# Three attentions by pairs of heads: V as the stationary operand in two column halves of TensorE, and probabilities divided before they are turned

## The reference, cut to what matters

```
scores = einsum("bqhd,bkhd->bhqk", q_blk, k) * scale      # 8 heads, 96 wide, 512 keys
scores = where(k_idx <= q_idx, scores, -inf)
probs  = softmax(scores, axis=-1)
out    = einsum("bhqk,bkhd->bqhd", probs, v)              # 64 wide
```

## Time and profile before

| what | us |
|---|---|
| median of three runs | 3442.46 (3441.18 to 3444.32) |
| profiled execution, in all | 3443.18 |
| its span, first to last instruction | 3441.5 |
| PE busy | 3358.2 (98%) |
| DVE, ACT, POOL busy | 1790.0, 1471.7, 1433.9 |
| mean granted TensorE clock | 0.997 of full speed |

### The profile page before, as it was taken

One profiled execution on the slowest core, in us unless ns is written; L12 is line 12 of the kernel. 1 busy time (PEld: TensorE's weight loads), 2 busy tenths in 40 slices (PEclk: granted clock), 3 DMA queues, 4 the chain that ended last, 5 costly groups with the idle time before them and its releaser, 6 DMA issues. The chain is left out here.

```text
span 3441.5 us, 49476 instructions
## 1 busy us (share of the span) xinstructions
PE 3358.2 (98%) x19319; PEld 2796.6 (81%) x19319; DVE 1790.0 (52%) x3313; ACT 1471.7 (43%) x2970; POOL 1433.9 (42%) x1268
## 2 busy tenths in 40 slices
PE   8999999999999899999999999999999999999999
PEld 7778778888877687888888878888888878888887
DVE  4655574636456674565463286455153186445243
ACT  4672354323344554532333347344343246544343
POOL 3320154454443545444544431345554432345543
PEclk9999999999999999999999999999999999999999
DMA  4210024545321122344443220222323220123321
GB/s 117 78 44 15 27 86 135 196 147 170 99 89 50 36 88 88 111 149 168 159 147 111 84 74 14 74 86 92 104 83 101 91 79 26 50 86 98 98 92 56
DMA packets 232836, 317.89 MB, mean 92 GB/s; under 512 B 9909, under 2 KB 149148, under 8 KB 232604
## 3 DMA queue, kind: packets, MB, share of 16 engines
q1 hardware_dynamic: 203206, 261.55, 23.6%
q10 hardware_dynamic: 29398, 53.17, 4.6%
HBM read 312.59 MB, written 2.10 MB: 91 GB/s over the span
## 5 line engine op out<-in xcount | busy, mean ns | idle before, releaser
L364 PE MATMUL banks<-split,split 128*128 128x512 f32 (+2 forms) x11760 | 2681.0, 389 | 24.2 <-ACT split L383 13.6
L364 PEld LDWEIGHTS banks<-split,split 128*128 128x128 f32 x11760 | 2185.3, 188 | 496.3 <-ACT split L383 24.5
L387 POOL TENSOR_TENSOR split<-kept,split 128x512 fp32r<-128x512 f32 (+2 forms) x1158 | 1356.8, 1176 | 1709.9 <-ACT split L383 1707.2
L383 ACT ACTIVATE split<-kept 128x512 fp32r<-128x512 f32 (+2 forms) x1158 | 646.3, 564 | 1454.3 <-PE banks L364 1408.0
L1590 DVE SCALAR_TENSOR_TENSOR work<-banks,kept,work 128x511 f32<-128x511 f32 (+1 forms) x176 | 120.5, 746 | 257.0 <-ACT work L1572 256.2
L910 DVE SCALAR_TENSOR_TENSOR work<-work,kept 128x512 f32<-128x512 f32 x168 | 194.5, 1158 | 6.0
L855 DVE SCALAR_TENSOR_TENSOR kept<-banks,kept 128x512 f32<-128x512 f32 x48 | 33.3, 746 | 209.6 <-PE banks L364 209.6
L853 DVE TENSOR_TENSOR kept<-banks,kept 128x512 f32<-128x512 f32 x64 | 40.6, 685 | 195.2 <-PE banks L364 195.2
L540 DVE COPY work<-banks 128x512 f32<-128x512 f32 (+1 forms) x64 | 37.4, 644 | 195.4 <-PE banks L364 195.3
L1165 PE MATMUL banks<-work 128*128 128x128 f32 x928 | 136.4, 277 | 1.0 <-ACT work L1241 0.6
L1165 PEld LDWEIGHTS banks<-work 128*128 128x128 f32 x928 | 118.6, 192 | 6.0 <-ACT work L1241 2.8
(11 more groups left out here) (413 smaller groups left out, 3079.8 us busy)
## 6 DMA issues: line engine op xcount, KB each, us to landing
work<-in_mod_w ACTq DMA_DIRECT2D x48, 1024.0 KB, 6.0
kept<-in_ffn_w SPq DMA_DIRECT2D x94, 512.0 KB, 4.8
kept<-in_w_up SPq DMA_DIRECT2D x88, 512.0 KB, 4.8
kept<-in_w_in SPq DMA_DIRECT2D x36, 1024.0 KB, 5.0
kept<-in_od_w_in SPq DMA_DIRECT2D x20, 1024.0 KB, 5.1
kept<-in_ffn_w SPq DMA_DIRECT2D x18, 1024.0 KB, 5.4
kept<-in_w_down SPq DMA_DIRECT2D x18, 1024.0 KB, 4.9
kept<-in_ev_w_in SPq DMA_DIRECT2D x8, 1024.0 KB, 5.1
```

The source lines that it names most:

```text
L364: m = pe.matmul(self.bank(q, j), lhs, rhs, start=t == 0 and i == 0, stop=t == job.KT - 1 and i == 2)
L383: act.activation(self.weights(s, 0), self.source(s), ACT.Copy).then_inc(self.rounded, 1)
L387: pool.tensor_tensor(self.weights(s, 1), self.source(s), self.weights(s, 0), ALU.subtract).then_inc(self.k.slices_split, 1)
```

## The change

A new class `PairedHeads` takes the place of `Attend` in the first attention, and `StackedHeads` now builds on it. The cross attentions keep `Attend`.

- Units go by pairs of heads: of eight units, u % 2 chooses the head and u % 8 // 2 the query block.
- `scores` run three units ahead of `turn_p` instead of two. There are four tiles of probabilities and four of turned ones.
- After the exponential VectorE takes the reciprocal, and GpSimd multiplies the probabilities by it in place (`divide`); `turn_p` waits for that.
- ScalarE takes the turned probabilities of t = 0 and 1 (`take_p`), VectorE those of t = 2 and 3 (`move_p`).
- `mix` runs once for two units. V is stationary, 64 columns, the turned probabilities move; the first head's output goes to partitions 0 to 63 of the bank, the second's to 64 to 127. The output comes out turned, so `out` and `turn_o` are gone, and four query blocks fill one bank.
- Queries (and keys) of the next pair are turned at fixed units of the present one (`TURN`), two heads ahead. The first two heads are turned at the start.
- In gate stages GpSimd rounds the query to its high half and subtracts for its low half (`stage_q`, two instructions) before the turn; `rest_q` is gone from VectorE. `begin_pool` stages two queries and a key instead of one of each. The aside moves to unit 12. Some tiles move in SBUF.

The new classes are cut here to the order of the work; the takes of queries and keys, tile and bank choices and the keys' halves are left out.

```diff
+class PairedHeads:
+
+    QB, KB, SB, TB, OB = 2, 3, (6, 7), (0, 1), (4, 5)
+    AHEAD = 3
+    TURN = (1, 3)
...
+    def place(self, u):
+
+        return u // 8 * 2 + u % 2, u % 8 // 2
...
+    def width(self, u):
+        return (self.place(u)[1] + 1) * P
...
+    def by_scalar(self, u):
+        return self.place(u)[1] < 2
...
+    def coming(self, u, steps):
+
+        h = u // 8 * 2 + 2
+        return [h + i for i in range(2) if h + i < len(self.heads) and steps[i] == u % 8]
...
+    def turn_p(self, pe, u):
+        pe.wait_ge(self.scaled, u + 1)
+        if u >= 2:
+            before = u - 2
+            if self.by_scalar(before):
+                pe.wait_ge(self.p_taken, self.count_taken(before))
+            else:
+                pe.wait_ge(self.p_moved, self.count_moved(before))
+        for c in range(self.place(u)[1] + 1):
+            m = pe.transpose(self.bank(self.TB[u % 2])[:, c * P:(c + 1) * P], self.prob[u % 4][:, c * P:(c + 1) * P],
+                             self.k.ident)
+        m.then_inc(self.p_turned, 1)
...
+    def mix(self, pe, m):
+
+        u = 2 * m
+        h, t = self.place(u)
+        if self.by_scalar(u):
+            pe.wait_ge(self.p_taken, self.count_taken(u + 1))
+        else:
+            pe.wait_ge(self.p_moved, self.count_moved(u + 1))
+        if t == 0 and h >= 4:
+            pe.wait_ge(self.o_ready, h // 2 - 1)
+        for c in range(t + 1):
+            for i in range(2):
+                ins = pe.matmul(self.o_bank(h // 2)[i * 64:i * 64 + 64, t * P:(t + 1) * P], self.heads[h + i].v(c),
+                                self.probT[(u + i) % 4][:, c * P:(c + 1) * P], start=c == 0, stop=c == t)
+        ins.then_inc(self.mixed, 1)
...
+    def go_on(self, pe):
+        for u in range(self.AHEAD):
+            self.scores(pe, u)
+        for u in range(self.units):
+            for h in self.coming(u, self.TURN):
+                self.turn_q(pe, h)
+                if self.new_keys(h):
+                    self.turn_k(pe, h)
+            if u + self.AHEAD < self.units:
+                self.scores(pe, u + self.AHEAD)
+            self.turn_p(pe, u)
+            if u % 2 == 0 and u:
+                self.mix(pe, u // 2 - 1)
+        self.mix(pe, self.units // 2 - 1)
+        self.k.keep_busy(pe, self.TB[0], 6)
...
+    def await_turned(self, eng, u):
+        eng.wait_ge(self.p_turned, u + 1)
+        if u >= 4:
+            eng.wait_ge(self.mixed, u // 2 - 1)
...
+    def take_p(self, act, u):
+        n = self.width(u)
+        self.await_turned(act, u)
+        act.activation(self.probT[u % 4][:, 0:n], self.bank(self.TB[u % 2])[:, 0:n], ACT.Copy).then_inc(self.p_taken, 1)
...
+    def go_on_scalar(self, act):
+        for u in range(self.AHEAD - 1):
+            self.exps(act, u)
+        for u in range(self.units):
+            if u + self.AHEAD - 1 < self.units:
+                self.exps(act, u + self.AHEAD - 1)
+            for h in self.coming(u, self.TURN):
+                self.take_q(act, h)
+                if self.new_keys(h):
+                    self.take_k(act, h)
+            if self.by_scalar(u):
+                self.take_p(act, u)
+            if u % 8 == 1 and u > 8:
+                self.round_o(act, u // 8 - 1)
+        self.round_o(act, self.units // 8 - 1)
...
+    def peak(self, dve, u):
+        h, t = self.place(u)
+        n = self.width(u)
+        dve.wait_ge(self.scored, u + 1)
+        if u >= 4:
+            dve.wait_ge(self.p_turned, u - 3)
+        dve.tensor_tensor_reduce(self.prob[u % 4][:, 0:n], self.bank(self.SB[u % 2])[:, 0:n], self.heads[h].mask(t), 1.0, -NEG,
+                                 ALU.add, ALU.min, self.top[:, u % 8:u % 8 + 1]).then_inc(self.peaked, 1)
...
+    def move_p(self, dve, u):
+        n = self.width(u)
+        self.await_turned(dve, u)
+        dve.tensor_copy(self.probT[u % 4][:, 0:n], self.bank(self.TB[u % 2])[:, 0:n]).then_inc(self.p_moved, 1)
...
+    def vector(self, dve, _link, q, c):
+        self.begin_vector(dve)
+        for u in range(self.AHEAD):
+            self.peak(dve, u)
+            if u:
+                self.invert(dve, u - 1)
+        for u in range(self.units):
+            if u + self.AHEAD < self.units:
+                self.peak(dve, u + self.AHEAD)
+            if u + self.AHEAD - 1 < self.units:
+                self.invert(dve, u + self.AHEAD - 1)
+            for h in self.coming(u, self.TURN):
+                if self.new_keys(h):
+                    self.rest_k(dve, h)
+            if not self.by_scalar(u):
+                self.move_p(dve, u)
+            if u % 8 == 2 and u > 8:
+                self.rest_o(dve, u // 8 - 1)
+            self.aside_vector(dve, u)
+        self.rest_o(dve, self.units // 8 - 1)
+        yield
...
+    def divide(self, pool, u):
+        tile = self.prob[u % 4][:, 0:self.width(u)]
+        pool.wait_ge(self.inverted, u + 1)
+        pool.tensor_scalar(tile, tile, self.inv[:, u % 8:u % 8 + 1], None, ALU.mult).then_inc(self.scaled, 1)
...
+class StackedHeads(PairedHeads):
+
+    ASIDE = 12
+    TURN = (1, 4)
+    STAGE_Q, STAGE_K = (0, 3), (1, 4)
...
     def stage_q(self, pool, h):
-        if h >= 1:
+        if h >= 2:
             pool.wait_ge(self.q_turned, h)
-        self.twice(pool, self.q_twice, self.heads[h].q).then_inc(self.q_staged, 1)
+        halves = self.q_places(h)
+        pool.tensor_copy(halves[:, :, 0:HD], self.heads[h].q).then_inc(self.q_halved, 1)
+        pool.wait_ge(self.q_halved, h + 1)
+        pool.tensor_tensor(halves[:, :, HD:P], self.heads[h].q, halves[:, :, 0:HD], ALU.subtract).then_inc(self.q_staged, 1)
...
     def pool(self, pool):
-        for h in range(1, len(self.heads)):
-            self.stage_q(pool, h)
-            if self.new_keys(h):
-                self.stage_k(pool, h)
+        for u in range(self.units):
+            for h in self.coming(u, self.STAGE_Q):
+                self.stage_q(pool, h)
+            for h in self.coming(u, self.STAGE_K):
+                if self.new_keys(h):
+                    self.stage_k(pool, h)
+            self.divide(pool, u)
...
-    attend = Attend(k, heads, QK ** -0.5, W(48), o_hi, o_lo, QK, V_MLA, lambda t: t + 1, ready, masked=True, idle_first=14)
+    tiles = [k.view(W(n), S) for n in range(46, 60)]
+    attend = PairedHeads(k, heads, QK ** -0.5, tiles[0:3], tiles[3:6], tiles[6:10], tiles[10:14], W(60), o_hi, o_lo, QK, ready,
+                         idle_first=14)
```

More of the change, by code:

```diff
@@ new lines, in turn_q, with turn_k @@
+    def turn_q(self, pe, h):
+        if h >= 2:
+            pe.wait_ge(self.q_ready, h)
+        for t in range(ST):
+            m = pe.transpose(self.q_bank(h)[:, t * P:(t + 1) * P], self.heads[h].q[:, t, :], self.k.ident)
+        m.then_inc(self.q_turned, 1)
+    def turn_k(self, pe, h):
+        if self.heads[h].keys >= 2:
+            pe.wait_ge(self.k_ready, self.heads[h].keys)
+        for t in range(ST):
+            m = pe.transpose(self.k_bank(self.heads[h].keys)[:, t * P:(t + 1) * P], self.heads[h].k[:, t, :], self.k.ident)
+        m.then_inc(self.k_turned, 1)
@@ new lines, in await_scores, with scores @@
+    def await_scores(self, pe, u):
+        h, t = self.place(u)
+        if t == 0:
+            pe.wait_ge(self.q_ready, max(h, 1) + 1)
+            pe.wait_ge(self.k_ready, self.heads[h].keys + 1)
+        if u >= 2:
+            pe.wait_ge(self.peaked, u - 1)
+    def scores(self, pe, u):
+        h, t = self.place(u)
+        n = self.width(u)
+        self.await_scores(pe, u)
+        pe.matmul(self.bank(self.SB[u % 2])[:, 0:n], self.q_tile(h)[0:self.dk, t * P:(t + 1) * P],
+                  self.k_tile(self.heads[h].keys)[0:self.dk, 0:n], start=True, stop=True).then_inc(self.scored, 1)
@@ L1409, in turn_k @@
         m.then_inc(self.k_turned, 1)
-    def turn_o(self, pe, p):
-        if (p + 1) * self.per * ST == self.ASIDE:
-            pe.wait_ge(self.aside.done, 1)
-        super().turn_o(pe, p)
     def scores(self, pe, u):
-        h, t = divmod(u, ST)
-        head, n = self.heads[h], self.keys(u)
-        if t == 0:
-            pe.wait_ge(self.q_ready, h + 1)
-            pe.wait_ge(self.k_ready, head.keys + 1)
-            if head.forget:
-                pe.wait_ge(head.forget.done, 1)
-        self.await_scores_bank(pe, u)
-        bank, q = self.bank(self.SB[u % 2])[:, 0:n], slice(t * P, (t + 1) * P)
-        pe.matmul(bank, self.qs[h % 2][:, q], self.kh[head.keys % 2][:, 0:n], start=True, stop=False)
+        h, t = self.place(u)
+        head, n = self.heads[h], self.width(u)
+        self.await_scores(pe, u)
+        if head.forget and t == 0:
+            pe.wait_ge(head.forget.done, 1)
+        bank, q = self.bank(self.SB[u % 2])[:, 0:n], self.q_tile(h)[:, t * P:(t + 1) * P]
+        high, low = self.k_tile(head.keys)
+        pe.matmul(bank, q, high[:, 0:n], start=True, stop=False)
         if head.forget:
```

202 lines of the change are left out of this document (152 added, 50 removed).

## The result

The changed kernel takes 3456.05 us (median of 6 runs, 3450.6 to 3457.47), beside it the kernel before 3441.91 (6 runs, 3440.34 to 3444.32): ratio 1.0037, 95% interval 1.0025 to 1.0049. So it is slower by 14 us, where 3428 was forecast. The profiled execution took 3457.47, its span is 3455.8, against 3443.18 and 3441.5.

The account below looks back on a forecast made before the run. TensorE, busy for 98% of the span, was taken as the bound. 33.8 us less work, some 16 lost to waits, left 18; minus 3.6 for openings gave 14.4 saved: 3428 us, range 3412 to 3441 (the forecast's own 3420 to 3435).

Parts of the forecast that it names:

- The mix and the turn of the output: TensorE's work in each attention pair: halves run together, mixes 1.25 us less; four output transposes go, 0.44 us less.
- the 33.8 forecast: TensorE's work over 20 attention pairs was to shrink by 33.8 us, 1.69 us a pair, before new waits.
- Rival 5: In the mixes the two halves run one after the other, 5.4 us a pair for 4.47: 3456 us; chance 2%.
- The hand schedule: Engine queues laid out by hand, with TensorE's waits: first attention, shared and forget pairs of 12.05, 10.3 and 12.15 us.
- the price of a divide: GpSimd's multiply of probabilities taken at its copy's price, 0.62 us at 512 columns, with 1.29 as the other end.
- Rival 4: GpSimd becomes the bound in gate-stage pairs, with divides of 2.0 us at 512: about 3461 us; chance 8%.
- The opening: Where gate stages open, GpSimd's longer staging adds 1.8 us, 3.6 in two stages; TensorE's wait becomes 2.8 us.
- That may cost up to 1.7 us more a stage: Half clock for 3.4 us behind each gate stage's opening wait could cost up to 1.7 us; left out of the sum.
- the ends' bound of 3 us: Where attentions begin and end, about 0.9 us against and 0.9 for: taken as zero, bounds -3 and +3.
- 18 us saved: Net gain in the three attentions: 4 x 1.13 + 8 x 0.5 + 8 x 1.17, after some 16 us go into waits.

Follow-up runs that it names:

- run 11: The changed kernel with GpSimd's subtraction for the low half of each query left out (one copy into both halves), no divide touched: 3442.51 us, a single run.
- the sides: The changed kernel with staging spread behind slices 1 to 3, 5 useless matmuls before each attention's first turn, and three small loads on SyncE: 3442.88 us.
- run 1: The changed kernel with the division of the probabilities left out, reciprocal still taken, outputs not normalised: 3433.4 us.
- run 5: The changed kernel with useless matmuls where TensorE waits, 12 at each gate stage's opening and 5 before each attention's first turn: 3450.45 us.
- run 13: The changed kernel with VectorE multiplying the 512-wide probabilities and ScalarE taking the 384-wide turned ones in exchange: 3437.1 us.
- run 7: The changed kernel with the three small loads behind the first attention issued on SyncE's queue instead of ScalarE's: 3452.57 us.
- run 8: The changed kernel with VectorE multiplying the 512-wide probabilities, GpSimd the other six units of eight: 3454.21 us.
- run 10: The changed kernel with VectorE multiplying the 512-wide probabilities, plus spread staging, matmuls without use before the first turns and small loads on SyncE: 3443.87 us.
- run 4: The changed kernel with all multiplications on VectorE, right behind the reciprocal, instead of on GpSimd: 3475.73 us.
- the best one: The changed kernel with VectorE's 512-wide multiplications, ScalarE's 384-wide copies, spread staging, useless matmuls before first turns and loads on SyncE: 3425.6 us, ratio 0.9936 to 0.9964.

## Why the prediction was wrong

- **The mix and the turn of the output: right.** Steps of two per 0.109, 0.16 at the end, 0.1 on entry. TensorE's busy time fell by 13.5 us while in the same two profiled executions (clocks of 0.997 and 0.993) the clock withheld some 14 more: about 27 of the 33.8 forecast are seen; the rest busy times don't tell, since the records overlap. Rival 5, the halves in single file, named 3456 us, which is what was measured, and is wrong all the same: a visit of eight records takes 0.59 us, not 0.88.
- **The hand schedule: near, for a kernel without the divide.** It gave 12.05, 10.3 and 12.15, the shared pair without the aside; without any divide they are 12.30, 9.79 and 12.10, and the attentions gain 3.4 + 8.2 + 8.2 = 19.8 us for the 18 forecast. It had a divide of 0.62 in it, which no run has, so in the first attention at least it was too hopeful. It also made too little of a dear divide: at 1.29 it gave 12.35, 10.8 and 12.2; at the 1.56 measured the pairs are 13.34, 11.05 (without the aside, in the first gate stage) and 12.67.
- **The step that failed: the price of a divide.** "A divide reads one tile, so I take the copy's price", 0.62 at 512, "and keep 1.29 as the other end". It takes 1.56, 0.60 at 128: about 0.28 us and 2.5 ns a column, more than the subtraction of two tiles. A pair's eight divides are 8.67 us of GpSimd where the copy's price makes 3.6, and TensorE waits for them before its turns, 9.7 us in one gate attention. No row of before had GpSimd multiply by a column, and the upper end was taken for a bound because it reads more. This is 22.7 us with what follows from it.
- **Rival 4 named the mechanism.** It had GpSimd pass a shared pair from 3.3 ns a column on; eight divides are 8.67 us for 2560 columns, 3.4 ns, by the fixed part that "1.7 us at 512" left out. It had the price at 512 too high (2.0), so that its 3461 us come out near by luck. GpSimd is full in the gate stages (93%), and run 11 shows that its load counts there. In the first attention it isn't full (8.62 of 13.34 us); there the longer chain costs 1.04 us a pair.
- **The opening: right in size, wrong in what hangs on it.** The waits are 2.88 and 2.82 us for the 2.8 forecast. "That may cost up to 1.7 us more a stage; it is not in the sum": it came at the first opening and not at the second, but in the whole kernel the clock withheld 9 to 12 us more than before. The starts of the attentions (1.08, 1.14 and 1.13 us for the first divide, of which the ends' bound of 3 us knew, taken as zero) and the late load, in no step of the prediction, bring stretches too. With cover at openings and starts the stretches there are gone while the waits stay.
- **Sum.** By the forecast's terms: 18 us saved became 1.5 us lost (50.81 + 95.38 + 95.50 for 48.56 + 95.81 + 95.84; some 1.4 of it is the stretch in the first attention), 3.6 us of opening came, and the other 9 of the 14 lie in the waits before the first turns and for the load and in what the clock withheld outside the attentions. The divide and the sides can be mended apart: 3433 - 3456 = -23, 3443 - 3456 = -13.

**What stays open.** Why the issue of rw_a takes 1.78 us. A transfer of 16 KB of instructions starts at 213.31 and lasts 1.40, a second of 8 KB at 213.30; in the kernel with the first attention alone 16 KB start at 212.40 (1.01 us) beside the slow issue of 1.41 at 212.38, and both issues end 0.36 and 0.38 us behind that transfer. Where only 8 KB or nothing falls beside it (before, runs 1, 5 and 13), the issue takes 0.61 to 0.67. It goes the same way on either queue: in nine of the traces, run 7 with its loads on SyncE among them, an issue of 1.02 to 2.03 us ends 0.30 to 0.38 behind a transfer of 16 KB; in two (runs 8 and 10) such a transfer began during the issues and they took 0.58 to 0.79. That speaks for waiting on instructions, but it wasn't tried by moving code. Open too is what decides whether a stretch at 0.5 follows a wait. After has two in stages that the change leaves alone (1092.7 and 1181.4 us), behind waits of 2.22 and 2.93 us; before has waits of 2.22 and 3.22 there and no stretch, but one of 6.83 us at 981 where after has 3.41. One or both lie in most versions, the best one too; neither lies in the kernel that changes the gate stages alone, nor in runs 4, 11 and 13, which change the first attention as well. So a few microseconds of the 14 hang on where such stretches happen to fall.

## What to carry to other kernels

Before work moves to GpSimd, look for its price for exactly that kind of operand; if no row has it, the dearest row of another kind is no upper bound, and the busy sum with twice that price must still fit the period. A new wait of a microsecond of TensorE may cost more than itself: look at the granted clock behind it, in more than one trace, and keep the engine busy or spread what it waits for. When one engine's queue is relieved at the cost of another's, give that one something back; the same multiplications on VectorE were worth 2 us alone, which is nothing that can be told, and 19 with two copies moved off it.

## What the runs showed of the hardware

- A multiply by a column of 128x512 f32, SBUF to SBUF: 1.56 us on GpSimd, 0.49 on VectorE (0.54 while GpSimd divides too), 0.71 on ScalarE. VectorE takes 0.487 for 384 columns as for 512.
- The Trainium skill (GPSIMD Engine Reference, Engine selection) calls one-input operations on GpSimd roughly line-rate; its copy of 512 was (0.61), its multiply by a column was not, three times VectorE's time. The measurement decides.
- Half clock came with waits of TensorE of 1.14 and 1.54 us, 3.4 and 10.2 us of it; waits of 1.04, 2.22 and 3.22 (before) and of 2.82 (after) had none. The wait for in_rw_g was followed by it at 0.82, 1.28, 1.54 and 1.70 us and not at 0.74, 0.87, 1.07 and 1.13, in eight versions.
- The issue of a DMA of 128 or 256 KB took 0.52 to 0.79 us, but one in each of nine traces, with 16 KB of instructions loading beside it, 1.02 to 2.03.
